# VectorE's one-column operations of three attentions, once for a pair of heads instead of once for each head

## The reference

```
# 1 "window": banded attention with a sink per head, latent queries over latent and context keys
sinks = jnp.broadcast_to(sink_col, s_win.shape[:-1] + (1,))
p = jax.nn.softmax(jnp.concatenate([s_win, s_ctx, sinks], axis=-1), axis=-1)
...
# 2 "ab": MoBA and dilated heads;  3 "nsa": selected and window keys, each softmax with a gate
m = jnp.max(s, axis=-1, keepdims=True)
e = jnp.exp(s - m)
l = jnp.sum(e, axis=-1, keepdims=True)
p = e / jnp.where(l > 0, l, 1.0)
...
o = (gates[..., 0:1] * o_cmp + gates[..., 1:2] * o_slc + gates[..., 2:3] * o_win)
```

## Time and profile before

| what | us |
|---|---|
| median of three runs (2652.51 to 2654.16) | 2653.35 |
| the profiled execution | 2657.53 |
| its span in the profile | 2655.4 |
| window attention, first bias to first matmul of the output projection | 1558.18 to 1623.95 |
| second attention (ab), the same | 1917.56 to 1980.85 |
| third attention (nsa), the same | 2331.10 to 2403.01 |

### The profile page before, as it was taken

The page is one execution under the profiler, slowest core; times in us unless marked ns, Lnnn a source line. Parts: engine busy times, 40 slices in busy tenths (PEclk is TensorE's granted clock), DMA queues, the critical chain, the costliest instruction groups (busy, mean ns, idle before and its releaser), DMA issues.

```text
span 2655.4 us, 40078 instructions
## 1 busy us (share of the span) xinstructions
PE 2531.2 (95%) x15799; PEld 2161.7 (81%) x15799; DVE 1362.7 (51%) x2130; ACT 1158.7 (44%) x1831; POOL 23.7 (1%) x37
## 2 busy tenths in 40 slices
PE   6999999998999999999999988999989998979998
PEld 4777787875777778777788767999869998869998
DVE  3323334895523333423333477555777665786665
ACT  3333323465433322433322356554456545565554
POOL 0000000000000000000000000000000001000000
PEclk7999999999999999999999899999989998989999
DMA  7444542210344433344422312454414554413553
GB/s 282 176 171 163 189 170 95 82 45 0 133 168 166 182 128 110 111 182 166 162 97 105 109 50 77 177 180 168 178 65 179 185 194 171 161 36 116 185 190 143
DMA packets 52725, 374.88 MB, mean 141 GB/s; under 512 B 5822, under 2 KB 7034, under 8 KB 8736
## 3 DMA queue, kind: packets, MB, share of 16 engines
q1 hardware_dynamic: 50000, 358.63, 36.6%
q0 software_dynamic: 2208, 14.37, 1.6%
q10 hardware_dynamic: 432, 0.73, 0.1%
HBM read 372.55 MB, written 7.39 MB: 143 GB/s over the span
## 4 chain that ended last, share of the span: by engine, by line
PE 89%; DVE 7%; ACT 2%; issue 1%; DMA 1%; SPq 0%; ACTq 0%; DVEq 0%
PE acc L1816 27%; PE acc L1817 26%; PE acc L1818 26%; PE bank L1893 3%; PE bank L1920 1%; DVE sc L1717 1%; DMA ada_raw<-in_slabs 1%; DVE wlo L1272 1%; DVE sc L1746 1%; ACT sc L1176 1%; DVE prod L584 1%; DVE prod L1634 0%; PE Mod L1903 0%; PE bank L1941 0%; PE acc L2270 0%
## 5 line engine op out<-in xcount | busy, mean ns | idle before, releaser
L1272 DVE TENSOR_TENSOR wlo<-raw,whi 128x1024 fp32r<-128x1024 f32 x534 | 646.8, 1223 | 911.5 <-ACT whi L754 910.9
L754 ACT ACTIVATE whi<-raw 128x1024 fp32r<-128x1024 f32 x534 | 555.9, 1055 | 974.7 <-PE acc L1818 917.8
L1816 PE MATMUL acc<-hhi,whi 128*128 128x256 f32 (+1 forms) x2808 | 951.7, 339 | 24.1 <-DVE hlo L1356 10.9
L1817 PE MATMUL acc<-hlo,whi 128*128 128x256 f32 (+1 forms) x2808 | 937.9, 334 | 0.0
L1818 PE MATMUL acc<-hhi,wlo 128*128 128x256 f32 (+1 forms) x2808 | 937.3, 334 | 0.0
L1816 PEld LDWEIGHTS acc<-hhi,whi 128*128 128x128 f32 x2808 | 541.2, 193 | 109.3 <-issue 55.3
L1818 PEld LDWEIGHTS acc<-hhi,wlo 128*128 128x128 f32 x2808 | 541.0, 193 | 50.8
L1817 PEld LDWEIGHTS acc<-hlo,whi 128*128 128x128 f32 x2808 | 541.5, 193 | 49.9 <-issue 1.7
L1816 PE MATMUL acc<-ghi,whi 128*128 128x512 f32 (+1 forms) x1056 | 357.1, 338 | 0.0
L1818 PE MATMUL acc<-ghi,wlo 128*128 128x512 f32 (+1 forms) x1056 | 357.0, 338 | 0.0
L1817 PE MATMUL acc<-glo,whi 128*128 128x512 f32 (+1 forms) x1056 | 357.0, 338 | 0.0
(11 more groups left out here) (267 smaller groups left out, 2266.9 us busy)
## 6 DMA issues: line engine op xcount, KB each, us to landing
raw<-in_slabs SPq DMA_DIRECT2D x331, 1024.0 KB, 4.8
ada_raw<-in_slabs SPq DMA_DIRECT2D x8, 1024.0 KB, 23.2
skew_dram<-lines_dram POOLq DMA_DIRECT2D x1, 6144.0 KB, 23.8
bt<-skew_dram POOLq DMA_DIRECT2D x4, 1024.0 KB, 8.9
x<-in_x_in SPq DMA_DIRECT2D x1, 2048.0 KB, 17.9
mlp<-in_slabs POOLq DMA_DIRECT2D x2, 1024.0 KB, 6.1
out<-x SPq DMA_DIRECT2D x1, 1024.0 KB, 4.8
rope<-in_rope POOLq DMA_DIRECT2D x1, 512.0 KB, 4.0
```

The lines of the kernel that those rows point to most:

```text
L754: nc.scalar.activation(whi[:, n % 2, cols], raw_of(n, cols), ACT.Copy).then_inc(ready, 1)
L1272: nc.vector.tensor_tensor(wlo[:, n % 2, cols], raw_of(n, cols), whi[:, n % 2, cols].bitcast(F32), ALU.subtract).then_inc(low, 1)
L1816: nc.tensor.matmul(out, w[0], xx[0], start=first, stop=False)
L1817: nc.tensor.matmul(out, w[0], xx[1], start=False, stop=False)
```

## The change

A new table `neg_sink` (128 x 16) holds the negatives of the sinks; it is made once at the start. `biased` and `normalised` are called once for a pair. `biased` makes the biased scores and maxima of both heads first, then one instruction for the negated maxima of both (in the window attention the minimum of the negated maximum and the negated sink, from the table). It raises `m_ready` once for a pair, and ScalarE's `exps` of either head waits for that. `normalised` waits until the exponentials of both heads are done (`e_ready` at u + 2), does the addition, the reciprocal and the gates once for both, and then scales both heads' rows. The loop over the pairs keeps its order.

```
--- before.py
+++ after.py
@@ -360,6 +360,7 @@
         eps_sq = sb("eps_sq", [P, 1])
         rs_tok = sb("rs_tok", [P, 4])
         two_gains = sb("two_gains", [P, DT])
+        neg_sink = sb("neg_sink", [P, NH])
 
 
         with ExitStack() as ffn:
@@ -1169,7 +1170,7 @@
 
                 def exps(u):
 
-                    act.wait_ge(m_ready, A0 + u + 1)
+                    act.wait_ge(m_ready, A0 // 2 + u // 2 + 1)
                     sp = stt4[:, u % 4]
                     keys = 512 if st.what == "window" else P * (rows_of(u) + 1)
                     for s in range(2 if st.what == "nsa" else 1):
@@ -1285,6 +1286,8 @@
                 for col in (VCOL["qk_gain_ab"], VCOL["qk_gain_nsa"]):
 
                     nc.vector.tensor_scalar(vec[:, col:col + 4], vec[:, col:col + 4], HD ** -0.5, None, ALU.mult)
+                s = VCOL["sink"]
+                step.done(nc.vector.tensor_scalar(neg_sink[:, :], vec[:, s:s + NH], -1.0, None, ALU.mult))
                 f, g = VCOL["final_g"], VCOL["norm_mix"]
                 step.done(nc.vector.tensor_tensor(two_gains[:, :], vec[:, f:f + DT], vec[:, g:g + DT], ALU.mult))
 
@@ -1707,63 +1710,61 @@
 
                 def biased(u):
 
-                    q, b = rows_of(u), u % 4
-                    sp = stt4[:, b]
+                    q, b, h = rows_of(u), u % 4, head_of(u)
                     keys = 512 if win else P * (q + 1)
-                    dve.wait_ge(s_ready, A0 + u + 1)
-                    dve.wait_ge(t_ready, A0 + u + 1)
-                    bias = mask[:, q, :] if win else bt[:, head_of(u), P * (1 - q):S]
-                    for s in range(2 if nsa else 1):
-                        ins = nc.vector.tensor_tensor_reduce(sc[:, b, keys * s:keys * s + keys],
-                                                             B[u % 4][:, keys * s:keys * s + keys], bias,
-                                                             1.0, LOWEST, ALU.add, ALU.max, sp[:, s:s + 1])
-                    ins.then_inc(s_free, 1)
-                    dve.wait_ge(s_free, 4 + A0 + u + 1)
+                    for v in (u, u + 1):
+                        dve.wait_ge(s_ready, A0 + v + 1)
+                        dve.wait_ge(t_ready, A0 + v + 1)
+                        bias = mask[:, q, :] if win else bt[:, head_of(v), P * (1 - q):S]
+                        for s in range(2 if nsa else 1):
+                            ins = nc.vector.tensor_tensor_reduce(sc[:, v % 4, keys * s:keys * s + keys],
+                                                                 B[v % 4][:, keys * s:keys * s + keys], bias,
+                                                                 1.0, LOWEST, ALU.add, ALU.max,
+                                                                 stt4[:, v % 4, s:s + 1])
+                        ins.then_inc(s_free, 1)
+                    dve.wait_ge(s_free, 4 + A0 + u + 2)
+                    w = 2 if nsa else 1
+                    top, low = stt4[:, b:b + 2, 0:w], stt4[:, b:b + 2, 2:2 + w]
                     if win:
-
-                        sink = VCOL["sink"] + head_of(u)
-                        ins = nc.vector.tensor_scalar(sp[:, 2:3], sp[:, 0:1], vec[:, sink:sink + 1], -1.0,
-                                                      ALU.max, ALU.mult)
+                        sinks = neg_sink[:, h:h + 2].rearrange("p (a b) -> p a b", b=1)
+                        ins = nc.vector.scalar_tensor_tensor(low, top, -1.0, sinks, ALU.mult, ALU.min)
                     else:
-                        w = 2 if nsa else 1
-                        ins = nc.vector.tensor_scalar(sp[:, 2:2 + w], sp[:, 0:w], -1.0, None, ALU.mult)
+                        ins = nc.vector.tensor_scalar(low, top, -1.0, None, ALU.mult)
                     ins.then_inc(m_ready, 1)
 
                 def normalised(u):
-                    q, b = rows_of(u), u % 4
-                    sp = stt4[:, b]
-                    dve.wait_ge(e_ready, A0 + u + 1)
+                    q, b, h = rows_of(u), u % 4, head_of(u)
+                    w = 2 if nsa else 1
+                    sums2, parts = stt4[:, b:b + 2, 4:4 + w], stt4[:, b:b + 2, 7:7 + w]
+                    dve.wait_ge(e_ready, A0 + u + 2)
                     if win:
-                        step.done(nc.vector.tensor_tensor(sp[:, 4:5], sp[:, 4:5], sp[:, 6:7], ALU.add))
-                    w = 2 if nsa else 1
-                    step.done(nc.vector.reciprocal(sp[:, 7:7 + w], sp[:, 4:4 + w]))
+                        step.done(nc.vector.tensor_tensor(sums2, sums2, stt4[:, b:b + 2, 6:7], ALU.add))
+                    step.done(nc.vector.reciprocal(parts, sums2))
                     if nsa:
-                        g = 3 * head_of(u) + 1
-                        step.done(nc.vector.tensor_tensor(sp[:, 7:9], sp[:, 7:9], gates[:, q, g:g + 2], ALU.mult))
+                        two = gates[:, q, 3 * h:3 * h + 6].rearrange("p (a b) -> p a b", b=3)
+                        step.done(nc.vector.tensor_tensor(parts, parts, two[:, :, 1:3], ALU.mult))
                     keys = 512 if win else P * (q + 1)
-                    for s in range(w):
-                        p = sc[:, b, keys * s:keys * s + keys]
-                        ins = nc.vector.tensor_scalar(p, p, sp[:, 7 + s:8 + s], None, ALU.mult)
-                    ins.then_inc(p_ready, 1)
+                    for v in (u, u + 1):
+                        for s in range(w):
+                            p = sc[:, v % 4, keys * s:keys * s + keys]
+                            ins = nc.vector.tensor_scalar(p, p, stt4[:, v % 4, 7 + s:8 + s], None, ALU.mult)
+                        ins.then_inc(p_ready, 1)
 
                 def out_lo(pair):
                     dve.wait_ge(o_hi, A0 // 4 + pair + 1)
                     nc.vector.tensor_tensor(olo[:, pair, :], out_bank(st, pair)[:, 0:S],
                                             ohi[:, pair, :].bitcast(F32), ALU.subtract).then_inc(o_lo, 1)
 
-                for u in range(4):
-                    biased(u)
+                biased(0)
+                biased(2)
                 normalised(0)
-                normalised(1)
                 for u in range(0, UNITS, 2):
                     if u + 2 < UNITS:
                         normalised(u + 2)
-                        normalised(u + 3)
                     if u % 4 == 0 and u > 4:
                         out_lo(u // 4 - 2)
                     if u + 4 < UNITS:
                         biased(u + 4)
-                        biased(u + 5)
                     if st.what == "ab" and 12 <= u < 20:
                         for c in (u - 12, u - 11):
                             g = VCOL["final_g"] + c
```

## The result

The changed kernel takes 2667.94 us (median of 4 runs, 2664.37 to 2672.15) against 2653.76 us of the kernel before: 14.2 us more, ratio 1.0055, 95% interval 1.0042 to 1.0067. It is slower, as forecast (2674.3 us, range 2666 to 2685), by two thirds of the 20.9 us of the sum, and 2 us inside the lower end of the range. Its profiled execution takes 2666.25 us, with a span of 2664.1 us (before 2657.53 and 2655.4).

The account below looks back on a forecast made before the run. The prediction took the attentions' ring of engines handing work to each other as the bound: window +11.5, third +3.2, +4.9 and +0.8, low halves +1.5, second -1, in sum +20.9 us, giving 2674.3 us, range 2666 to 2685.

Parts of the forecast that it names:

- the 20.9 us of the sum: Whole kernel: predicted slowdown, 11.5 + 3.2 + 4.9 + 0.8 + 1.5 - 1 us.
- The lost stagger: Attentions: VectorE and ScalarE no longer work on different heads at once; +0.96 us a window pair, +0.81 or +1.22 in the third.
- low halves: Six rounds, two window and four third, with a weight slab's low part behind the bias: 0.25 us each, +1.5 in sum.
- the prologue: Window attention's first two pairs: the second pair's bias covers the first pair's exponentials; taken as 0.
- the start-up step: First 15 us: one more 128x16 instruction, under 0.25 us, ahead of all weights; taken as 0.
- Rival 1: All three attentions: saved instructions count, waits do not; 21.6 us faster, 2631.8 us; chance 0.05.
- ScalarE's chain: Attentions: a pair's exponentials on ScalarE, 1.88 us in the window attention, 1.65 or 2.08 in the third.
- Rival 2: Attentions: TensorE closes the ring and its slack takes up the added wait; no change, 2653 us; chance 0.05.
- Rival 3: Attentions and projection starts: longer gaps lower TensorE's clock from 2.4 to 1.2 GHz; +14 us, 2688 us; chance 0.08.

Follow-up runs that it names:

- Each hand-over alone: Changed kernel with only the negated maximum paired: 2658.04 us, ratio 1.0017; with only sink addition, reciprocal and gate paired: 2648.56 us, ratio 0.9979.
- gap_only: Kernel before plus an unused 64-byte tile where the change puts its table, all instructions the same: 2645.33 us, ratio 0.9966.
- the second profile: The changed kernel run and profiled once more without any edit: 2668.88 us, ratio 1.0051.
- the head-by-head kernel in the other order: Changed kernel with the bias of pair u+4 ahead of the normalisation of pair u+2, one-column operations head by head as before: 2668.04 us, ratio 1.0055.
- the swapped order: Changed kernel, everything paired, with the bias of pair u+4 ahead of the normalisation of pair u+2: 2647.32 us, ratio 0.9979.
- gap_weights: Kernel before plus an unused 64-byte tile ahead of the raw, high and low weights: 2648.46 us, ratio 0.9976.
- gap_all: Kernel before plus three unused 64-byte tiles, ahead of hhi, the raw weights and ghi: 2644.24 us, ratio 0.9968.

## Why the prediction was right, and where it was not

- **The lost stagger, +0.96 us a window round**: 4.66 us measured, 4.65 forecast; idle time before the addition 1.96 us (some 1.9), put down to the sink's exponential. Third attention 4.04 and 5.28 us (4.04 and 5.26). Each hand-over alone gave the round that the same sum gives for it. The second of two bias instructions started with the first one's accumulator read, 0.61 us after it, as taken.
- **The stages**: window +13.7 and +11.9 us (12.0 with its low halves), third +10.4 and +10.6 (9.9), second -2.9 and -0.5 (-1). In sum +21.2 and +22.0 (20.9). The single terms were a little less exact than their sum: the distances from bias to bias in the window attention grew by 0.96 us in 11 of 15, but by 0.12 in the first round, which I had counted with 0.96, and fell by 0.25 in the prologue, which I had taken as 0; the last pair's share lies behind its bias.
- **What failed is the zero for the start-up step.** I costed the new table as an instruction ("under 0.25 us") and not as an allocation. It moved every tile behind it by 64 bytes, which gained some 8 us in the down stages and 10.5 in the whole time of gap_only. That is in the main why the time came out 6.4 us under the forecast with attentions as long as forecast. The code shows the allocation; no row of before tells its price.
- **Rival 1** (saved instructions count) was wrong for this order. Its condition, other work as long as ScalarE's chain behind the bias, was the right one: where an order supplied it, pairing gained 20 us. That this is near the 21.6 worked out for it is luck: a plain window round gained 0.24 to 0.29 us, not 0.51, and the rest lies in the rounds held up by the low part, in the other attentions and outside all three.
- **Rival 2** (TensorE takes it up) fell. **Rival 3** (clock) is there in part: in the last 8 us of the changed window attention the mean granted clock was 0.70, eight transposes there took 1.97 us, the time at 1.2 GHz, and the whole attention's mean was 0.90 for 1.00. In the second profile the means are 0.85 and 0.96 and the attention is 1.8 us shorter, with the same rounds.

The Trainium skill, "Perfetto Trace Analysis", section "Optimizing Scalar/DVE Operations", says that grouping into larger operations can improve throughput if the engine is saturated. Here that doesn't decide: VectorE was busy for 56.2 of 65.8 us in before's window attention, where grouping lost, and for 55.1 of 75.3 in that of the head-by-head kernel in the other order, where grouping gained.

## What to carry to other kernels

Merging two instructions also merges their waits: before counting what is saved, look what the engine has queued between the hand-over and its answer. If nothing, first put another unit's work there (and look whom that delays); then merging can pay, as it did in the swapped order here. And treat a new small tile as a move of all tiles behind it: compare the matmul count of a fully busy stretch, and keep the layout fixed with an unused tile when testing anything else.

## What the runs showed of the hardware

- At a granted clock of 1.00 and busy throughout, TensorE's pace on alternating weight tiles depends on the distance of streamed operand and weights in SBUF. At 256 columns: 169 to 171 in 20 us at a distance of 0 modulo 128 bytes, 178 or 179 at 64. At 512 columns: 90 (in one profile 89) at a multiple of 256 bytes, 87 or 88 at others. The Trainium skill, "TensorE: Matmul & The Clock Gate", section "Step-by-step: what each phase is for", has the next weights load without taking read bandwidth from the running matmul. The counts do not show who is slowed, but the pace isn't independent of the distance here. Why, no run tells; other element sizes weren't tried.
- The same code of the third attention takes 71.9 us in both profiles of before at a clock of 0.87, 67.9 in gap_only and 68.0 in gap_weights at 0.92, and 71.6 in gap_all at 0.89. So a stage with gaps can differ by 4 us with its granted clock and no other instruction. What decides it, no run tells: the attention starts at 2325.0 us in gap_only and at 2325.8 in gap_all.
